# Feed-forward rounding ahead of the activations' copy, memory tiles in the layer norm, and GpSimd splitting the down-projection tiles

## What is computed

```python
def conformer_conv(u, b_glu, w_dw, b_dw, ln_g, ln_b):
    u = u + b_glu
    a, gate = jnp.split(u, 2, axis=-1)
    v = a * jax.nn.sigmoid(gate)
    v = causal_dwconv(v, w_dw, b_dw)          # 31 taps
    v = layernorm(v, ln_g, ln_b)
    return jax.nn.silu(v)

def conv_ffn(h, w_up, w_dw, b_dw, w_down):
    u = h @ w_up                              # 1024 -> 2 x 2816
    u = causal_dwconv(u, w_dw, b_dw)          # 3 taps
    gate, val = jnp.split(u, 2, axis=-1)
    return (jax.nn.silu(gate) * val) @ w_down # 2816 -> 1024

def first_block(x, mem, ...):
    mem_n = rmsnorm(mem, g_mem)
    for l in range(DEPTH):                    # DEPTH = 2
        h = rmsnorm(x, g_mix[l])
        mem_k, mem_v = jnp.split(mem_n @ w_mem_kv[l], 2, axis=-1)
        if l < N_A:
            p = h @ w_in_a[l]
            u, q_mem = p[..., :2 * CONV_CH], p[..., 2 * CONV_CH:]
            mix = conformer_conv(u, ...)
        else:
            ...
            mix = forgetting_attention(q, k_sh, v_sh, cum_logf).reshape(bsz, seq, MIX_WIDTH)
        mem_o = memory_attention(q_mem, mem_k, mem_v)
        x = x + jnp.concatenate([mix, mem_o], axis=-1) @ w_out[l]
        x = x + conv_ffn(rmsnorm(x, g_ffn[l]), ...)
```

## Time and profile before

| | before |
|---|---|
| runs, us | 1386.06, 1378.59, 1384.35 (median 1384.35) |
| profiled execution, us | 1379.86 |
| its span from first to last instruction, us | 1378.1 |
| mean granted TensorE clock | 0.962 |
| PE busy | 1262.9 us (92%) |
| PEld busy | 1122.8 us (81%) |
| DVE busy | 892.6 us (65%) |
| ACT busy | 640.7 us (46%) |
| POOL busy | 11.6 us (1%) |
| DMA, mean over the span | 144 GB/s |

### The profile page before, as it was taken

How to read it: one execution, slowest core, us unless ns; L and a number is a source line. 1 busy time by engine, 2 the same in 40 slices (tenths; PEclk the granted TensorE clock), 3 DMA queues, 4 the chain that set the end, 5 groups by cost and what they waited for, 6 DMA issues and landing times.

```text
span 1378.1 us, 19422 instructions
## 1 busy us (share of the span) xinstructions
PE 1262.9 (92%) x8046; PEld 1122.8 (81%) x8046; DVE 892.6 (65%) x1361; ACT 640.7 (46%) x999; POOL 11.6 (1%) x27
## 2 busy tenths in 40 slices
PE   4989599999979999999997999979899999998897
PEld 4987499899869778989996977758798989997685
DVE  4996367777764656777777856555576646666454
ACT  5446454455553334444445334424444545555343
POOL 0000000000000000000000000000000000000000
PEclk8999799999999999999999999989999999999899
DMA  8440044444533323454443544424545623222241
GB/s 337 156 151 0 31 153 153 171 170 180 184 122 123 110 88 109 153 184 176 172 175 122 213 153 164 176 111 153 184 156 190 235 102 107 107 93 92 88 157 61
DMA packets 28135, 198.44 MB, mean 144 GB/s; under 512 B 3216, under 2 KB 3344, under 8 KB 4752
## 3 DMA queue, kind: packets, MB, share of 16 engines
q1 hardware_dynamic: 28048, 197.21, 39.6%
HBM read 196.14 MB, written 1.05 MB: 143 GB/s over the span
## 4 chain that ended last, share of the span: by engine, by line
PE 59%; DVE 20%; issue 10%; ACT 9%; DMA 1%; DVEq 0%; SPq 0%; POOL 0%; ACTq 0%; POOLq 0%
PE bank L677 15%; PE bank L678 15%; PE bank L679 15%; ACT WH L1149 7%; DVE WL L1497 7%; DVE work L1637 3%; DVE work L1633 3%; PE bank L943 2%; PE bank L1123 1%; DVE work L1681 1%; DVE work L1641 1%; DVE work L1629 1%; PE bank L1103 1%; PE bank L881 1%; DMA RAW<-wstream 1%
## 5 line engine op out<-in xcount | busy, mean ns | idle before, releaser
L1497 DVE TENSOR_TENSOR WL<-RAW,WH 128x2048 fp32r<-128x2048 f32 x181 | 414.0, 2289 | 245.4 <-ACT WH L1149 244.9
L1149 ACT ACTIVATE WH<-RAW 128x2048 fp32r<-128x2048 f32 x181 | 343.4, 1908 | 195.3 <-PE bank L679 183.1
L677 PE MATMUL bank<-XH,WH 128*128 128x256 f32 x1264 | 362.0, 286 | 12.3 <-DVE XL L1533 7.7
L678 PE MATMUL bank<-XL,WH 128*128 128x256 f32 x1264 | 358.8, 284 | 0.0
L679 PE MATMUL bank<-XH,WL 128*128 128x256 f32 x1264 | 358.5, 284 | 0.0
L677 PEld LDWEIGHTS bank<-XH,WH 128*128 128x128 f32 x1264 | 243.5, 193 | 16.9 <-DVE XL L1533 8.1
L678 PEld LDWEIGHTS bank<-XL,WH 128*128 128x128 f32 x1264 | 243.7, 193 | 0.5
L677 PE MATMUL bank<-WH,MH 128*128 128x512 f32 (+1 forms) x544 | 206.4, 379 | 40.8 <-DVE ML L1646 14.2
L679 PEld LDWEIGHTS bank<-XH,WL 128*128 128x128 f32 x1264 | 243.6, 193 | 0.0
L678 PE MATMUL bank<-WL,MH 128*128 128x512 f32 (+1 forms) x544 | 202.2, 372 | 0.0
L679 PE MATMUL bank<-WH,ML 128*128 128x512 f32 (+1 forms) x544 | 202.1, 372 | 0.0
(11 more groups left out here) (254 smaller groups left out, 1561.0 us busy)
## 6 DMA issues: line engine op xcount, KB each, us to landing
RAW<-wstream SPq DMA_DIRECT2D x181, 1024.0 KB, 4.8
con<-consts SPq DMA_DIRECT2D x1, 1681.0 KB, 17.9
x<-x_in SPq DMA_DIRECT2D x1, 1024.0 KB, 5.0
work<-mem_in SPq DMA_DIRECT2D x1, 1024.0 KB, 14.4
out_dram<-xn SPq DMA_DIRECT2D x2, 512.0 KB, 2.7
par<-params SPq DMA_DIRECT2D x1, 868.0 KB, 6.3
gfree<-g_final SPq DMA_DIRECT2D x1, 512.0 KB, 18.7
xn<-p_in SPq DMA_DIRECT2D x2, 256.0 KB, 3.8
```

What stands on the lines that cost most here:

```text
L677: mm(o, ah, bh, start=start, stop=False)
L678: mm(o, ah, bl, start=False, stop=False)
L1149: act_fn(WH[:, t % RING, :], RAW[:, t % RING, :], ACT.Copy).then_inc(w_rounded, 1)
L1497: tt(WL[:, t % RING, :], RAW[:, t % RING, :], WH[:, t % RING, :].bitcast(F32), ALU.subtract).then_inc(w_split, 1)
```

## The change

It has three parts.

1. In the feed-forward steps s = 2 to 9, ACT issues the rounding of the step's third tile (fd s-1) ahead of the copy of `fa` into MH rather than behind it. On DVE the call of the step's last `upto_n` moves behind ML in the last step (s = 10).
2. The 22 down-projection tiles (fd, 11 in each of the two feed-forward parts) are split by GpSimd instead of DVE. A second semaphore counts these, and PE and SP wait on the one that belongs to the tile.
3. The memory's keys and values of layer 1 (tiles mk 1 and mv 1) are multiplied and copied out in the layer norm: keys between the mean and the variance, values between the variance and the tiles o0. The normalized memory is kept in the upper half of MH and ML (KH, KL) for that.

The order of the tiles in the ring, the matmuls and all loads stay as they are.

```diff
+POOL_TILES = [t for t, key in enumerate(TILES) if key[0] == "fd"]
+DVE_TILES = [t for t, key in enumerate(TILES) if key[0] != "fd"]
...
+        def wait_split(eng, t):
+            if t in POOL_TILES:
+                eng.wait_ge(w_split_pool, POOL_TILES.index(t) + 1)
+            else:
+                eng.wait_ge(w_split, DVE_TILES.index(t) + 1)
...
             def load(t):
                 if t >= RING:
-                    sp.wait_ge(w_split, t - RING + 1)
+                    wait_split(sp, t - RING)
...
-            for n in (1, 0, 2, 3, 4):
+            def split(l):
+                for s in range(FSTEP):
+                    t = TILE[("fd", l, s)]
+                    pool.wait_ge(w_rounded, t + 1)
+                    nc.gpsimd.tensor_tensor(WL[:, t % RING, :], RAW[:, t % RING, :], WH[:, t % RING, :].bitcast(F32),
+                                            ALU.subtract).then_inc(w_split_pool, 1)
+
+            for n in (1, 0, 2):
                 rms(n)
+            split(0)
+            for n in (3, 4):
+                rms(n)
+            split(1)
...                                                   # PE
-                gemm_t(("mk", l), MH, ML, 0 if l == 0 else None)
-                gemm_v(("mv", l), MH, ML)
+            gemm_t(("mk", 0), KH, KL, 0)
+            gemm_v(("mv", 0), KH, KL)
...                                                   # PE, behind the mean
+            gemm_t(("mk", 1), KH, KL)
             o = take(("var",))
...                                                   # PE, behind the variance
+            gemm_v(("mv", 1), KH, KL)
             o = [take(("o0", q)) for q in range(4)]
...                                                   # ACT, feed-forward
+                    if LAG <= s < FSTEP - 1:
+                        upto_n(at + 3)
                     act.wait_ge(*dve_a.next())
                     m = 2 * (s % 4)
                     act_fn(MH[:, m:m + 2, :], fa[:, e, :].rearrange("p (b t) -> p b t", b=2), ACT.Copy).then_inc(hi_done, 1)
-                    if s >= LAG:
+                    if s == FSTEP - 1:
                         upto_n(at + 3)
...                                                   # DVE, feed-forward
-                    if s >= LAG:
+                    if LAG <= s < FSTEP - 1:
                         upto_n(at + 3)
                     dve.wait_ge(*hi_a.next())
                     m = 2 * (s % 4)
                     tt(ML[:, m:m + 2, :], fa[:, e, :].rearrange("p (b t) -> p b t", b=2),
                        MH[:, m:m + 2, :].bitcast(F32), ALU.subtract).then_inc(lo_done, 1)
+                    if s == FSTEP - 1:
+                        upto_n(at + 3)
```

More of the change, by code:

```diff
@@ L182, in plan_banks @@
     norm_full(0)
-    for l in range(2):
-        gemm(("mk", l), "act")
-        gemm(("mv", l), "act")
+    gemm(("mk", 0), "act")
+    gemm(("mv", 0), "act")
     for b in PE_CONV:
@@ L189, in plan_banks @@
     aux("B", ("mean",), "dve")
+    gemm(("mk", 1), "act")
     aux("B", ("var",), "dve")
+    gemm(("mv", 1), "act")
     acc("o0", ("o0", 3))
@@ L460, in program @@
         w_split = sem("w_split")
+        w_split_pool = sem("w_split_pool")
         w_used = sem("w_used")
@@ L524, in B @@
             return bank[USES.bank[key]]
-        norms = {0: [(MH, ML, "g_mem")], 1: [(XH, XL, "g_mix0")], 2: [(XH, XL, "g_ffn0")],
+        norms = {0: [(KH, KL, "g_mem")], 1: [(XH, XL, "g_mix0")], 2: [(XH, XL, "g_ffn0")],
                  3: [(KH, KL, "g_kv"), (XH, XL, "g_mix1")], 4: [(XH, XL, "g_ffn1")], 6: [(XH, XL, "gret")],
@@ L670, in tile @@
                 tiles[0] += 1
-                pe.wait_ge(w_split, t + 1)
+                wait_split(pe, t)
                 return WH[:, t % RING, :], WL[:, t % RING, :]
@@ L1295, in _ @@
             high(0, 1)
-            for l in range(2):
-                projected(("mk", l), mkt[:, l, :, :])
-                projected(("mv", l), mvv[:, l, :, :])
+            projected(("mk", 0), mkt[:, 0, :, :])
+            projected(("mv", 0), mvv[:, 0, :, :])
             for n, (b, k) in enumerate(pe_taps):
@@ L1312, in _ @@
             act_fn(lnsq, conv, ACT.Square).then_inc(act_for_pe, 1)
+            projected(("mk", 1), mkt[:, 1, :, :])
             act.wait_ge(*dve_a.next())
@@ L1325, in _ @@
                 act_fn(MH[:, c, :], conv[:, c, :], ACT.Copy, scale=0.5).then_inc(hi_done, 1)
+            projected(("mv", 1), mvv[:, 1, :, :])
             for c in range(3):
@@ L1495, in upto_n @@
                     n_split[0] += 1
+                    if t in POOL_TILES:
+                        continue
                     dve.wait_ge(w_rounded, t + 1)
@@ L1720, in _ @@
             low(0, 1)
[L1721 to L1724, removed]
+            for n in ("mk", "mv"):
+                upto((n, 0))
+                taps(8)
             dve.wait_ge(sw_rounded, 1)
@@ L1741, in _ @@
             free(dve.drain(), ("mean",), "dve")
+            upto(("mk", 1))
             ready(dve, ("var",))
@@ L1758, in _ @@
                 low_signal()
+            upto(("mv", 1))
             for c in range(2):
```

## The result

The changed kernel takes 1390.57 us (median of 20 runs, 1384.62 to 1394.07); the kernel before, run beside it, 1381.54 us (20 runs, 1376.78 to 1386.12). The ratio is 1.0055, with a 95% interval of 1.004 to 1.007: slower by 9.0 us by the medians and by 7.6 by the ratio, at the edge of the 0.5% that the prediction takes for the least that one measurement can tell. The forecast was 1385. The profiled executions have spans of 1385.4 and 1378.1 us, 7.3 apart.

A forecast was written before the change was run, and what follows sets the result against it. A ring of ScalarE and VectorE, 17.77 us per feed-forward step against PE's 17.0, was taken as the bound. Terms -10.6 + 11.4 = +0.8 on the profiled 1379.9 gave 1380.7, plus 4.5 to the median: 1385; range 1340 to 1399.

The forecast's parts named there:

- the middle: Feed-forward parts: the value taken between case A and case B, +5.7 us per part, +11.4 us in all.
- case A: Feed-forward steps: GpSimd's split stops VectorE at the first tap gap; ring 18.9 us, +10.8 per part; rival 1397, chance 0.27.
- case B: Feed-forward steps: GpSimd gets in only where VectorE waits for the copy into MH; ring 17.6 us, +0.5 per part.
- step 1: First feed-forward step: a VectorE split leaves, a GpSimd one stands in the way; +1.7 us in case A and case B.
- step 2: Second feed-forward step, which had no split in this place: +4.5 us in case A, 0 in case B.
- steps 3 to 9: Seven middle feed-forward steps: 7 x 1.13 = +7.9 us in case A, 7 x -0.17 = -1.2 in case B.
- step 10: Last feed-forward step, two GpSimd splits in place of two VectorE ones: +0.7 us in case A, +4.0 in case B.
- ML ahead: Last feed-forward step: ML moves in front of the next tile's split; -4.0 us per part in case A and case B.
- The ring: Feed-forward step's chain of ScalarE and VectorE from one copy into MH to the next: 17.77 us before, 14.4 without conflict.
- Part 3: Layer norm: two memory tiles moved there start diagonals and convolution 11.5 us earlier, variance ends 0.9 later; -10.6 us.
- the rival of tiles that don't fit: Layer norm: at a low clock the keys take 11.5 us and push the variance; only -5 us; chance one in ten.
- No conflict: Feed-forward steps: GpSimd's split never delays VectorE, PE sets the step; -17 us per part, 1340 in all; chance 0.20.

The follow-up runs named there:

- e_late: Changed kernel, but GpSimd begins the splits of fd 1 to fd 8 only after VectorE's join of the step's activations; 1371.73 us, 0.9912 of the kernel before.
- e_parts13: Changed kernel with all 22 down-projection splits back on VectorE, none on GpSimd; 1336.12 us, 0.9648 of the kernel before.
- e_idle_tt: Changed kernel with all splits on VectorE, plus 22 GpSimd two-input subtractions on constants that nobody uses; 1413.56 us, 1.0222 of the kernel before.
- e_pool_ln: Changed kernel without the rounding ahead and with the earlier VectorE order at the end; GpSimd keeps its splits; 1395.95 us, 1.0093 of the kernel before.
- e_idle_one: Changed kernel with all splits on VectorE, plus 22 unused GpSimd one-input multiplications by a constant; 1393.8 us, 1.0069 of the kernel before.

## Why the prediction was right or wrong

- **What bounds the kernel: right.** PE's own step was worked out as 17.0; with the rounding ahead and the splits on VectorE the copies come every 16.98 us.
- **GpSimd's operation: right.** 4.6 us was taken between bounds of 2.29 and 10.5; it is 4.60. The rows before gave the bounds alone: a factor of two in between was a choice, and that it hit so closely isn't owed to them.
- **The conflict: the step that failed.** The forecast took "the middle, +5.7 per part" between A (+10.8) and B (+0.5). The parts cost +10.0 and +10.2: case A, in every step. A middle between two mechanisms describes neither. B wanted DVE's taps to run on until DVE waits for a copy. But GpSimd is ready at 266.96, just as DVE passes from L1658 to the first tap, and gets in ahead of that tap. e_late shows case B: 17.70 us (17.6 predicted), a first part of 211.01 us in place of 211.14 (-0.1, priced +0.5). In these runs it took a wait to get there.
- **Case A's own terms were right.** Step by step, from the copies at 201.48, 217.48 and 236.28 and so on: step 1 +1.6 (predicted +1.7), step 2 +4.4 (+4.5), steps 3 to 9 +7.3 (+7.9), step 10 +0.4 (+0.7), ML ahead -3.8 (-4.0). The ring is 18.81 (18.9).
- **Part 3: right, 0.8 us too good.** -9.8 against -10.6. The copy is at 85.24, so the diagonals start 11.1 and not 11.5 us earlier; the variance starts at 138.46 behind the keys and still runs at the full clock (2.75 us), so the rival of tiles that don't fit is out. o0 starts at 152.63, its first matmuls as slow as before (0.77).
- **"No conflict": right in price, wrong in its condition.** 1340 was the price of a split that costs the ring nothing. e_parts13 runs at 1336 with the split on VectorE. What I missed is that the conflict-free place was VectorE's own: with its split of 2.29 us the ring is 15.2 us, under PE's 17.0, while GpSimd's stop makes it 14.4 + 4.4 = 18.8.
- **The sum.** The forecast was +0.8. Case A as priced is +11, and with its measured parts -9.8 + 10.0 + 10.2 = +10.4, near the +9.0 of the medians. The error is the middle value, 2 x (10.8 - 5.7) = 10.2 us, less the 2 us by which case A was priced above the medians. That 1385 lies only 5.6 us under 1390.57 is luck in part: the forecast started from 1384.35 for the kernel before, whose median over 20 runs is 1381.5. And the range of 1340 to 1399 took in nearly every case, so that the result lies in it says little about the mechanism: the one that came true had been given a chance of 0.27.
- **Not foreseen**: PE waits for GpSimd directly at two places, 1.4 us for the first tile of the part and 3.1 us for the tile before the last (the third row of the waits), where a rounding comes late. The wait for the last ML stays, at 5.1 us, as a conflict was to leave it.

## What to carry to other kernels

Before an operation goes to GpSimd, look at which VectorE operations will be running when its input becomes ready: if they read two operands from SBUF and it reads too, nearly its whole duration is added to VectorE's list (4.44 of 4.62 us with two inputs, 3.45 of 5.37 with one), so a split of 2.29 us there becomes a stall of 4.4. A VectorE row that has grown without its shape changing (1516 against 480 ns) was waiting here, not working, and the timeline of GpSimd at the same moment names for what. And undo a change part by part: here one part was worth -36 us alone, another -12 to -16, and the third took back 55.

## What the runs showed of the hardware

- The exclusion works both ways, and back-to-back VectorE operations don't keep GpSimd out: it enters at the boundary between two of them (208.67/208.78/210.88 above), ahead of an operation issued 0.02 us before it too (266.94/266.96).
- What counts is how many inputs VectorE reads from SBUF. In e_idle_tt the scaling, which multiplies PSUM by a row in SBUF, ran at its usual 0.68 us inside a GpSimd operation of 4.71, and the split behind it had to wait (6.08). Eight scalings beside a GpSimd operation, in e_late, e_pool_ln, e_idle_tt and e_idle_one, all show 0.68 or 0.69:

```profile
377.09 4.71 POOL L643 TENSOR_TENSOR work<-con 128x2048 f32<-128x2048 f32 x1 [4.85 <-ACT WH L1176]
377.28 0.68 DVE L1597 TENSOR_TENSOR work<-bank,rb 128x512 f32<-128x512 f32 x1
377.88 6.08 DVE L1529 TENSOR_TENSOR WL<-RAW,WH 128x2048 fp32r<-128x2048 f32 x1
```

- GpSimd on 128 x 2048: two inputs 4.53 to 4.62 us in the first part of the changed kernel, one input 5.37 at the least, of which it holds VectorE 3.45; only writing 1.81 or 1.82, with no hold. Why one input is slower than two, and lets go early, wasn't tried.
